# Two blocks of a transformer in one program: mask matmuls interleaved, and two reorderings in ScalarE's queue

## The reference

```
# differential: two softmaxes of one head (m = 0, 1), subtracted
logits = einsum(q, k) * scale + bias;  p = softmax(logits)
attn = p[:, :, 0] - lam * p[:, :, 1];  out = attn @ v
# sparse: keys outside the top 256 of an index score are masked
logits = einsum(q, k_sel) * scale - slope * dist;  out = softmax(logits) @ v_sel
# forgetting: a decay from the running sum of log sigmoid(f)
logits = einsum(q, k) * scale + cum_f[q] - cum_f[k];  causal mask
out = softmax(logits) @ v
```

## Time and profile before

| what | value |
|---|---|
| median of three runs | 3109.51 us |
| the profiled execution | 3109.51 us, span 3107.7 us |
| granted TensorE clock, mean | 0.984 |
| TensorE matmul busy | 2972.1 us (96%) |
| VectorE busy | 1341.1 us (43%) |
| ScalarE busy | 632.5 us (20%) |
| GpSimd busy | 1391.0 us (45%) |

### The profile page before, as it was taken

One profiled execution on the slowest core, in us unless ns is written; L12 is line 12 of the kernel. 1 busy time (PEld: TensorE's weight loads), 2 busy tenths in 40 slices (PEclk: granted clock), 3 DMA queues, 4 the chain that ended last, 5 costly groups with the idle time before them and its releaser, 6 DMA issues.

```text
span 3107.7 us, 33232 instructions
## 1 busy us (share of the span) xinstructions
PE 2972.1 (96%) x13502; PEld 2205.1 (71%) x13509; DVE 1341.1 (43%) x2012; ACT 632.5 (20%) x1056; POOL 1391.0 (45%) x814
## 2 busy tenths in 40 slices
PE   7999989889999999999999898999998999999997
PEld 4544446557888888888788556677667888887886
DVE  0499957646522325434414653111313433234323
ACT  1411026531100001111211462101112211111111
POOL 2000000045666666665677003444445666666663
PEclk9999989999999999999999999999999999999999
DMA  4111126232333333333433002332333332333331
GB/s 99 35 34 41 34 79 188 82 118 87 89 112 99 90 101 101 120 97 95 116 94 95 14 1 56 87 123 67 82 104 120 88 102 89 102 94 122 94 102 62
DMA packets 364920, 273.22 MB, mean 88 GB/s; under 512 B 14049, under 2 KB 334817, under 8 KB 364769
## 3 DMA queue, kind: packets, MB, share of 16 engines
q1 hardware_dynamic: 357568, 253.30, 28.5%
q10 hardware_dynamic: 4720, 10.68, 0.9%
q0 software_dynamic: 2480, 7.13, 0.7%
HBM read 262.59 MB, written 8.49 MB: 87 GB/s over the span
## 4 chain that ended last, share of the span: by engine, by line
PE 87%; DVE 4%; DMA 3%; issue 2%; POOL 2%; ACT 1%; SPq 0%; DVEq 0%; ACTq 0%; POOLq 0%
PE PS L809 39%; PE PS L821 24%; PE PS L761 5%; PE PS L775 4%; DMA ring<-in_w_in 3%; PE PS L446 3%; PE PS L1013 2%; PE PS L881 2%; PE PS L464 2%; PE PS L484 1%; POOL w_low L1883 1%; PE PS L476 1%; PE PS L895 1%; DVE arena L550 1%; PE PS L738 1%
## 5 line engine op out<-in xcount | busy, mean ns | idle before, releaser
L1883 POOL TENSOR_TENSOR w_low<-ring,w_high 128x1024 fp32r<-128x1024 f32 x382 | 939.0, 2458 | 31.9
L1880 POOL TENSOR_SCALAR w_high<-ring 128x1024 fp32r<-128x1024 f32 x382 | 426.1, 1115 | 1023.2 <-PE PS L821 369.9
L821 PE MATMUL PS<-w_high,hid_high 128*128 128x512 f32 x864 | 337.2, 390 | 9.1 <-issue 9.1
L821 PE MATMUL PS<-w_high,hid_low 128*128 128x512 f32 x864 | 336.6, 390 | 0.0
L821 PE MATMUL PS<-w_low,hid_high 128*128 128x512 f32 x864 | 336.6, 390 | 0.0
L809 PE MATMUL PS<-hT_high,w_high 128*128 128x512 f32 x656 | 272.5, 415 | 13.8 <-POOL w_low L1883 13.8
L809 PE MATMUL PS<-x1T_high,w_high 128*128 128x512 f32 x704 | 275.6, 391 | 3.5 <-DVE x1T_low L1574 3.5
L809 PE MATMUL PS<-x1T_low,w_high 128*128 128x512 f32 x704 | 275.1, 391 | 0.0
L809 PE MATMUL PS<-x1T_high,w_low 128*128 128x512 f32 x704 | 274.9, 391 | 0.0
L809 PE MATMUL PS<-hT_high,w_low 128*128 128x512 f32 x656 | 257.4, 392 | 0.0
L809 PE MATMUL PS<-hT_low,w_high 128*128 128x512 f32 x656 | 257.2, 392 | 0.0
(11 more groups left out here) (268 smaller groups left out, 4617.9 us busy)
## 6 DMA issues: line engine op xcount, KB each, us to landing
ring<-in_w_ff SPq DMA_DIRECT2D x128, 512.0 KB, 3.8
ring<-in_w_in SPq DMA_DIRECT2D x112, 512.0 KB, 3.9
ring<-in_w_gu SPq DMA_DIRECT2D x88, 512.0 KB, 3.9
ring<-in_w_ada SPq DMA_DIRECT2D x48, 512.0 KB, 4.9
ring<-in_w_down SPq DMA_DIRECT2D x44, 512.0 KB, 3.6
ring<-in_w_out SPq DMA_DIRECT2D x32, 512.0 KB, 4.4
ring<-in_w_branch SPq DMA_DIRECT2D x16, 512.0 KB, 3.9
arena<-in_x SPq DMA_DIRECT2D x8, 512.0 KB, 8.3
```

The costliest lines, as they stand in the source:

```text
L821: mm = pe.matmul(PS[:, 2 * p + half, :], x[:, k, at], w[:, q, half_of(half)], start=(first and n == 0), stop=(last and n == 2))
L1880: pool.tensor_scalar(w_high[:, q, :], ring[:, s, :], 1.0, 1.0, ALU.mult, ALU.mult).then_inc(weights_high, 1)
L1883: pool.tensor_tensor(w_low[:, q, :], ring[:, s, :], w_high[:, q, :].bitcast(F32), ALU.subtract).then_inc(weights_used[s], 1)
```

## The change

Three edits. In `scores`, the mask or decay matmul of a map now follows directly on that map's product, and stands ahead of the other map's product and its wait; before, both products came first. In ScalarE's loop, exps(u+1) now stands ahead of copy_turned(u-1), in all three attentions. Before forget, copy_v2(1) now stands ahead of the wait for `cum_done` and of the two casts.

```
@@ Attention.pe, scores
                     for c in range(0, N, 512):
                         w = min(512, N - c)
-                        more = [None if self.more is None else self.more(pe, u, m, c, w) for m in range(2)]
                         for m in range(2):
                             if c == 0 and u >= 1:
                                 pe.wait_ge(self.logits_made, 2 * u - 1 + m)
+                            more = self.more(pe, u, m, c, w) if self.more is not None else None
                             mm = pe.matmul(PS[:, 2 * m + c // 512, 0:w], self.q(j, m, b), self.k(j, m, c, w),
-                                           start=True, stop=more[m] is None)
-                            if c + w == N and more[m] is None:
+                                           start=True, stop=more is None)
+                            if more is not None:
+                                mm = pe.matmul(PS[:, 2 * m + c // 512, 0:w], *more, start=False, stop=True)
+                            if c + w == N:
                                 mm.then_inc(self.scores_done, 1)
-                        for m in range(2):
-                            if more[m] is not None:
-                                mm = pe.matmul(PS[:, 2 * m + c // 512, 0:w], *more[m], start=False, stop=True)
-                                if c + w == N:
-                                    mm.then_inc(self.scores_done, 1)
@@ Attention.act
                 for u in range(last + 2):
+                    if u < last:
+                        exps(u + 1)
                     if u >= 1:
                         copy_turned(u - 1)
-                    if u < last:
-                        exps(u + 1)
@@ ScalarE's queue before forget
                 copy_tiles("qk2", 1, u, qk2T)
+            copy_v2(1)
             act.wait_ge(cum_done, 1)
             for r in (slice(0, 8), slice(64, 72)):
                 act.copy(cum_r[r, :], fl[0:8, :]).then_inc(cum_high, 1)
-            copy_v2(1)
             forget.act(act)
```

## The result

The changed kernel takes 3198.9 us, the median of four runs (3195.68 to 3201.08), against 3109.63 for the kernel before beside it (3108.42 to 3110.59): a ratio of 1.0286, with a 95% interval of 1.0269 to 1.0304. It is slower by 89 us, where 60 were forecast, and it lies 7 us above the range. The profiled execution has a span of 3195.9 us against 3107.7, and a mean granted clock of 0.970 against 0.984. In the attention code every line number is three lower than before: L443 to L446 is the product of queries and keys, L449 the mask or the decay, L461 the transposes, L473 and L481 the product with the values, L507 the exponentials, L521 the copies, L547 the logits; L1078, L1263, L1716 and L1723 are the copy of v2, the casts, the subtraction and the windows.

The account below looks back on a forecast made before the run. TensorE, busy 96% of the span, was taken to set the pace. Terms 18 (seam) + 16 + 5 (sparse) + 0 + 18 (forget) + 3 (diff) = 60 on 3109.5 gave 3170 us, range 3142 to 3192.

Parts of the forecast that it names:

- Seam: Between v2 and forget: casts behind copy_v2(1) leave VectorE's chain hidden by nothing; +18 us (17 to 22).
- Masks in sparse: Sparse scores: a 128-row mask between the two products makes them run in line; +20.4 us of TensorE, net +16.
- my 4: Sparse: map 0's logits start earlier, so TensorE's stops for logits shrink by about 4 us.
- Rival A: Forget: the two maps no longer run abreast; +31 us of TensorE less about 11, total 3190; chance 0.13.
- Exps ahead of the copies: Attention stages: copies queue behind exps(u+1), so TensorE waits; +18 us in forget, +5 in sparse, +3 in diff.
- forget's sites: Forget, copies behind blocks 1, 5, 3 and 7 come late: +1.0, +0.65, +1.5 and, between heads, +1.85 us.
- My 5: Sparse: late copies cost about +5 us (0 to 9), since map 0 being ready earlier eats most delays.
- one site: Block b=1: its logits and exps delay block 7's third transpose job by +1.0 us.
- what I gave back (2.5): Diff: VectorE's waits for exps go, giving TensorE back 2.5 us, within the net +3.
- part 3: ScalarE's exps(u+1) ahead of copy_turned(u-1): +18 us in forget, about +5 in sparse, +3 in diff.
- part 2: Mask or decay matmul behind each product: net +16 us in sparse, 0 in forget, 0 in diff.

Follow-up runs that it names:

- the filled kernels: Changed kernel plus throwaway matmuls fitted to TensorE's stops in sparse and forget: 3185.35 us; with every stop of sparse filled, 3172.71 us.

## Why the prediction was partly wrong

**Seam: right.** 18 forecast, +17.6 in the changed trace, +18.9 in the median of its own kernel. (The rule of the Trainium skill, SBUF — State Buffer, section Who interferes with whom, that the prediction weighed is borne out: the same four instructions take 0.78 with GpSimd idle and 4.49 with it at work.)

**Masks in sparse: right in mechanism.** The pair grew to 2.75 as worked out. The edit alone cost the stage 15.2 for 16, but the program 10.9 by its median. At full clock, on top of the second edit, it is 109.0 - 98.7 = 10.4 (unrounded), so part of the 15.2 was clock already (0.95), or the idle left gave back more than my 4.

**Rival A: wrong, as I held.** The maps stay abreast (1.19 us from one chunk to the next, rows above). That its bound was 3200 and 3198.9 was measured is chance. (The Trainium skill, TensorE: Matmul & The Clock Gate, section The mechanism, has matmuls strictly in order; neither trace bears it out.)

**Exps ahead of the copies: the stops right in forget, short in diff, not settled in sparse.** Forget has +5.0 in each j, as forecast. Sparse shows +8.1 at full clock for the second edit alone; the prices of forget's sites give 2 x 3.15 + 1.85 = 8.15 there. My 5 was for both edits together, with the masks hiding a part, and for both the stage shows +18.5 where 16 + 5 = 21 was forecast; how that divides is not shown. At one site I was short: of ScalarE's extra work I had not counted the table load that now stands in front of the copies, and the stop grew by 1.64 where I had 1.0. Diff cost 4.8 to 6.2 for 3. Its stops for copies rose to 8.6 us in twelve, from 0.7 in one, while 3.5 us of stops for VectorE's store went, so 4.4 more. Its waits for logits stayed at 2.8 us, so what I gave back (2.5) did not come.

**The step that failed** is the sum of part 3 with part 2: it prices each stop at its own length and each matmul at what its row shows at full clock. A stop of 1 to 3.6 us cost that, and then up to some 14 us of TensorE's work behind it ran at half speed. The earlier trace rows had the sign of it (0.95 in forget), and so had the 2.08 us behind the stop of 1.95; the prediction put the clock at nothing without a reason. The matmuls of sparse were busy 35.4 us longer, when the masks' serialising asks for at most 20.4. Worked out of the windows: with levels of 1 and 0.5, a stretch of length T at a mean granted clock c spends 2 x (1 - c) x T at the lower one, and loses at most half of that, (1 - c) x T; in sparse 0.18 x 129.4 = 23.3 against 0.02 x 90.5 = 1.8 before, in forget 0.12 x 179.9 = 21.6 against 0.05 x 150.1 = 7.5. That is 36 us more, of which the filled kernels got back 20.4 and 12 to 13. With this fits that two edits cost more together than apart: sparse keeps 0.95 and 0.89 with one of them, and 0.82 with both. What exactly in TensorE's work makes the clock fall at one stop and not at another stays open.

With the stops of sparse and forget filled the sum is 17.6 + 18.5 + 17 + 4.8 = 58, and 60 was forecast. That this is so near is in part luck: sparse came out 2.5 lower and diff 1.8 higher than forecast. The missing term was about 33 less the 3 that the rest of the span gave back.

## What to carry to other kernels

Before pricing a new stop of TensorE, read the granted clock of the stage, and look at how long the matmuls behind its present stops take. Here a stop of 3.59 us was followed by some 13 us at half speed, so it could cost up to 6 us more than its length, and two edits cost 74.8 together where they cost 55.6 apart. The most that the clock can cost is half of the time that the stretches behind the new stops would spend at the lower level. In a queue that goes in order, what nobody needs yet (exps of the next unit) belongs behind what an engine waits for (the copies), and a table load that it brings with it counts too.

## What the runs showed of the hardware

- Useless matmuls in TensorE's stops made the kernel faster: 65 more in sparse, 129.4 to 109.0 us. Ten in each of the larger stops gained nothing (3202.15 against 3198.9, with intervals that overlap), so the number has to be fitted to the stop.
- The clock stays at its lower level for a while although the engine is wholly busy again (654 to 662 in the changed kernel, 4.00 of 4.00 us at 0.50).
- A stage's busy share does not tell its clock: sparse is busy 82% of the time before, at 0.98, and 85% after, at 0.82.
- With useless matmuls in forget, the part of the program behind it took 1228.2 to 1234.7 us, without them 1223.5 to 1230.3; the cause is open.
- Matmuls on different halves of the rows overtake others across product and decay, in both orders of the code (1.19 us for a pair of 512 columns either way); with one matmul over all 128 rows between them they do not: 1.59 us for a pair becomes 2.75.
